# Six of eight rows of four down projections as pairs of seven products, and pairs that split two blocks at once

## The chip, the core and the metric

The kernel runs on one core of a Trainium2 chip. Its time is the device time of one execution in microseconds. Five engines work side by side: TensorE multiplies, ScalarE and VectorE prepare its operands and take its results out of PSUM, SyncE (SP) starts the plain weight loads, and GpSimd (POOL) starts those loads that are added to what is already in the buffer.

## The reference

One layer of each of two blocks, in float32, on 512 tokens of width 1024. What matters here are three feed-forward parts:

```python
def swiglu(x, w_gu, w_down):          # twice in the first block, D_FF = 2816
    g, u = jnp.split(x @ w_gu, 2, axis=-1)
    return (jax.nn.silu(g) * u) @ w_down
...
        x = x + jnp.square(jax.nn.relu(h @ w_up[l])) @ w_down[l]   # second block, width 4096
```

Between and around them stand a gated convolution, gated linear attention, neighbourhood attention, retention and norms, which keep their arithmetic.

## The kernel before

All activations lie transposed: 128 features on the partitions, 512 tokens along the row. Each float32 product is made of three float32r matmuls: the weight is split into a high part (`wh`, a cast on ScalarE, `hi`) and a low part (`wl`, a subtraction on VectorE, `lo`), the activation into `Ahi` and `Alo`, and high by high, high by low and low by high are added up in PSUM.

The work is a fixed list of units. A plain unit is one row of 128 outputs: eight blocks of 128 inputs, three matmuls of 512 tokens each, so 24. A *pair* is two rows at once. Its weights are taken as a 2 by 2 matrix of blocks (two rows, two halves of the inputs), the activations as another (two halves of the inputs, two halves of the tokens), and the product is made with seven block products instead of eight: `pair` on TensorE runs c = 0 to 6, each four inputs deep, with three matmuls of 256 tokens, so 84. The seven weight operands are a block, a sum s1, a sum s2, a block, a sum s3, a sum s4, a block. POOL loads s1 and s3 straight from memory, with a second load added on the way (`weight_sums`); VectorE makes s2 and s4 (`total`). `pair_hi` and `pair_lo` split one operand each, in 512 columns.

The results of a pair are collected in three PSUM banks. ScalarE copies three of them out on the way (`tap`, which TensorE waits for before it adds the next product into the same bank: c = 2 waits for tap 0, c = 4 for tap 2), VectorE adds others to the copies (`merge` 0 to 2; c = 6 waits for merge 1).

The gate and up projections of the FFNs, from the eighth (FFN 1) or sixth (FFN 2) row on, three gate projections of the mixer, and three of the four groups of the MLP's up projection run as pairs. For them the activation side is a normed input that is fixed for the whole layer, so the seven activation operands (`BThi`, `BTlo`) are built once ahead. The down projections run as plain units. An FFN works in groups of eight, eight and six hidden blocks (`FG`), the MLP in four groups of eight: up rows first, then eight down units that add into X.

In the MLP a pair gives two rows of hidden units. The first row's ReLU and square (`TA[3]`, `TA[4]`) follow merge 2, the second row's right half follows merge 1, and its left half follows the last product: `second_left` (a ReLU on ScalarE) stands in the *next* pair's queue, ahead of `tap(p, 0)`. `high` and `a_lo` split the result into `Ahi` and `Alo`.

Every engine's queue is written out by hand and runs in order; semaphores join them: `wh`, `wl` for splits, `pe` for products, `tp` for taps, `ev` for merges, `sd` for the sums, `ah`, `al` for activation splits. Weight buffers are a ring: three raw tiles, three tiles of high and three of low parts, each tile two half slots of 512 columns.

## Time and profile before

| | us |
|---|---|
| median of 3 runs | 1752.6 (1752.58 to 1753.64) |
| profiled execution | 1752.49 |
| its span, first to last instruction | 1750.3 |
| TensorE busy | 1743.7 |
| VectorE busy | 1180.2 |
| ScalarE busy | 847.5 |
| POOL busy | 201.8 |

The profile follows one execution. A row of a timeline gives the start, the duration, the engine, the line, what is written from what, the shape, how many instructions were merged into it, and in brackets how long the engine stood idle before it and what ended that. The shown duration of one instruction overlaps the next one's start by about a tenth of a microsecond, and matmul durations show the whole pipeline, so the distance between starts tells what an instruction costs its queue.

### The profile page before, as it was taken

The page shows a single profiled execution, that of the slowest core. Times are in us where ns is not written, and L with a number is a line of the kernel's source. Part 1 is how long each engine was busy: PE and PEld are TensorE (multiplying, and loading weights), DVE is VectorE, ACT ScalarE, POOL GpSimd, SP SyncE. Part 2 cuts the span into 40 slices and gives each one's busy share as a digit, 9 for nine tenths or more (in the row PEclk, how much of TensorE's full clock was granted, in tenths as well). Part 3 has the DMA queues.
Part 4 walks back from the last instruction along what each step waited for, and adds up shares of the span by engine and source line. Part 5 has one row for each costly group of instructions (what it writes and reads, how often), then busy time and mean ns, then how long its engine had stood idle before and what let it go on. Part 6 is the DMA issues. An engine that isn't in the chain of part 4 may idle for free.

```text
span 1750.3 us, 26650 instructions
## 1 busy us (share of the span) xinstructions
PE 1743.7 (100%) x10407; PEld 1534.1 (88%) x10407; DVE 1180.2 (67%) x1843; ACT 847.5 (48%) x1442; POOL 201.8 (12%) x262
## 2 busy tenths in 40 slices
PE   9999999999999999999999999999999999999998
PEld 7889989878888899988888998988877888989897
DVE  7848748666776546865794784876688677747474
ACT  6425526454333335743553562654655543727274
POOL 1002201000001012200110220200232010202000
PEclk9999999999999999999999999999999999999999
DMA  7247736332125355733445573634522253637352
GB/s 224 79 139 173 195 97 157 110 108 86 51 85 155 97 145 154 175 107 98 136 121 152 147 193 111 167 100 133 139 62 61 85 144 97 161 109 185 100 133 72
DMA packets 85451, 220.66 MB, mean 126 GB/s; under 512 B 10800, under 2 KB 12080, under 8 KB 85328
## 3 DMA queue, kind: packets, MB, share of 16 engines
q1 hardware_dynamic: 58512, 156.92, 29.1%
q0 software_dynamic: 25536, 59.97, 16.0%
q10 hardware_dynamic: 1280, 2.08, 0.3%
q8 instruction: 83, 1.36, 0.3%
q14 instruction: 40, 0.33, 0.1%
HBM read 214.74 MB, written 2.10 MB: 124 GB/s over the span
## 4 chain that ended last, share of the span: by engine, by line
PE 97%; DVE 1%; ACT 0%; issue 0%; DMA 0%; DVEq 0%; ACTq 0%; POOLq 0%
PE ps L2101 19%; PE ps L2103 19%; PE ps L2102 19%; PE ps L2193 10%; PE ps L2195 10%; PE ps L2194 10%; PE ps L2123 2%; PE ps L2125 2%; PE ps L2124 2%; PE ps L2342 0%; PE ps L2472 0%; PE ps L2497 0%; PE ps L2483 0%; PE ps L2345 0%; PE ps L2330 0%
## 5 line engine op out<-in xcount | busy, mean ns | idle before, releaser
L2101 PE MATMUL ps<-Ahi,wh 128*128 128x512 f32 x913 | 357.1, 391 | 0.0
L2102 PE MATMUL ps<-Alo,wh 128*128 128x512 f32 x913 | 355.3, 389 | 0.0
L2103 PE MATMUL ps<-Ahi,wl 128*128 128x512 f32 x913 | 355.3, 389 | 0.0
L2193 PE MATMUL ps<-BThi,wh 128*128 128x256 f32 x1232 | 340.2, 276 | 0.0
L2194 PE MATMUL ps<-BTlo,wh 128*128 128x256 f32 x1232 | 340.1, 276 | 0.0
L2195 PE MATMUL ps<-BThi,wl 128*128 128x256 f32 x1232 | 340.1, 276 | 0.0
L585 ACT ACTIVATE wh<-raw 128x1024 fp32r<-128x1024 f32 (+1 forms) x206 | 213.2, 1036 | 221.1 <-PE ps L2103 187.1
L1203 DVE TENSOR_TENSOR wl<-raw,wh 128x1024 fp32r<-128x1024 f32 (+1 forms) x206 | 250.2, 1215 | 64.4 <-ACT wh L585 62.3
L2194 PEld LDWEIGHTS ps<-BTlo,wh 128*128 128x128 f32 x1232 | 231.3, 188 | 0.0
L2193 PEld LDWEIGHTS ps<-BThi,wh 128*128 128x128 f32 x1232 | 231.3, 188 | 0.0
L2195 PEld LDWEIGHTS ps<-BThi,wl 128*128 128x128 f32 x1232 | 231.2, 188 | 0.0
L2103 PEld LDWEIGHTS ps<-Ahi,wl 128*128 128x128 f32 x913 | 171.4, 188 | 35.8
L2101 PEld LDWEIGHTS ps<-Ahi,wh 128*128 128x128 f32 x913 | 171.4, 188 | 35.7 <-issue 0.2
L2102 PEld LDWEIGHTS ps<-Alo,wh 128*128 128x128 f32 x913 | 171.4, 188 | 35.4 <-issue 0.2
L2101 PE MATMUL ps<-Hhi,wh 128*128 128x512 f32 x494 | 195.7, 396 | 0.0
L2103 PE MATMUL ps<-Hhi,wl 128*128 128x512 f32 x494 | 192.4, 390 | 0.0
L2102 PE MATMUL ps<-Hlo,wh 128*128 128x512 f32 x494 | 192.4, 389 | 0.0
L597 ACT ACTIVATE wh<-raw 128x512 fp32r<-128x512 f32 x168 | 105.0, 625 | 66.9 <-PE ps L2103 40.2
L1210 DVE TENSOR_TENSOR wl<-raw,wh 128x512 fp32r<-128x512 f32 x168 | 114.9, 686 | 7.8 <-ACT wh L597 6.5
L1294 DVE TENSOR_TENSOR tm<-ps,tm 128x256 f32<-128x256 f32 x168 | 71.0, 423 | 71.7 <-PE ps L2195 58.4
L2101 PEld LDWEIGHTS ps<-Hhi,wh 128*128 128x128 f32 x494 | 92.8, 188 | 22.1 <-issue 2.9
L2103 PEld LDWEIGHTS ps<-Hhi,wl 128*128 128x128 f32 x494 | 92.7, 188 | 19.6
(398 smaller groups left out, 2802.9 us busy)
## 6 DMA issues: line engine op xcount, KB each, us to landing
raw<-in_w_gu SPq DMA_DIRECT2D x96, 256.0 KB, 3.1
raw<-in_w_d SPq DMA_DIRECT2D x32, 512.0 KB, 4.2
raw<-in_w_dn SPq DMA_DIRECT2D x32, 512.0 KB, 4.1
raw<-in_w_gu SPq DMA_DIRECT2D x22, 512.0 KB, 3.8
raw<-in_w_up SPq DMA_DIRECT2D x36, 256.0 KB, 2.9
SS<-in_w_gu POOLq DMA_DIRECT2D x32, 256.0 KB, 5.1
tm<-in_w_gu POOLq DMA_DIRECT2D x32, 256.0 KB, 4.0
S1B<-in_w_gu POOLq DMA_DIRECT2D x32, 256.0 KB, 5.1
```

What stands on the lines that cost most here:

```text
L585: act.activation(WH[WS[u]][:, 0:n], RAW[RSL[u]][:, 0:n], ACT.Copy).then_inc(s["wh"], 1)
L597: act.activation(WHP[WS[p][c]], part(p, c), ACT.Copy).then_inc(s["wh"], 1)
L1203: dve.tensor_tensor(WL[WS[u]][:, 0:n], RAW[RSL[u]][:, 0:n], f32(WH[WS[u]][:, 0:n]), ALU.subtract).then_inc(s["wl"], 1)
L1210: dve.tensor_tensor(WLP[i], part(p, c), f32(WHP[i]), ALU.subtract).then_inc(s["wl"], 1)
L1294: dve.tensor_tensor(dst, BK[BANK[p][b]][:, LEFT], kept, ALU.add).then_inc(s["ev"], 1)
L2101: pe.matmul(ps, wh[:, c], hi[:, k, :], start=(k == 0), stop=False)
L2102: pe.matmul(ps, wh[:, c], lo[:, k, :], start=False, stop=False)
L2103: last = pe.matmul(ps, wl[:, c], hi[:, k, :], start=False, stop=(k == nb - 1))
L2123: pe.matmul(ps, Hhi[:, k, tc], wh[:, c], start=(k == 0), stop=False)
L2193: pe.matmul(ps, whi[:, w], bhi, start=(new and kp == 0), stop=False, skip_group_check=not new)
L2194: pe.matmul(ps, whi[:, w], blo, start=False, stop=False, skip_group_check=not new)
L2195: last = pe.matmul(ps, wlo[:, w], bhi, start=False, stop=(kp == 3), skip_group_check=not new)
```

## The change

The down projections of both FFNs' second group, and of the MLP's second and third groups, keep two plain rows and run the other six as three pairs. Their activation operands cannot be built ahead: the hidden blocks only arise in the up stage just before. Neighbouring blocks (0 and 1, 2 and 3, ...) take the two halves, so that a set can be built as soon as two blocks are there; the weights are laid out accordingly (`_mixed`, `column`). For each of four sets VectorE makes four blocks (`turned_ends`, `turned_middle`), ScalarE casts them (`turned_hi`), VectorE subtracts (`turned_lo`). In the FFNs these steps are spread over the up pairs 2 to 7 of the group and the first two down rows. In the MLP's pairs that begin at rows j = 2, 4 and 6 of a group VectorE makes the sums between `a_lo` of the second activation and merge 2, and ScalarE casts between the ReLU of the second row and that of the first. The fourth set is built during the first down row.

In all pairs the sums s1 and s2 lie beside each other, and so do s3 and s4, and each couple is split by one cast and one subtraction of 1024 columns: five steps (`STEP`) instead of seven. The ring of split weights grows from three tiles to four, temporaries shrink from nine to eight, and two FFN activations alternate between two temporaries. The space for descriptors of POOL's loads is halved. In every pair the casts stand in a new order around the taps.

```diff
-NW = 3
-NTMP = 9
+NW = 4
+NTMP = 8
...
+STEP = (0, 1, 1, 2, 3, 3, 4)
+NS = 5
+DOWN = ("w_d1", "w_d2", "w_dn")
+MIXED = (1, 2)
...
-                add(dn, n, a, b, 7)
+                add(dn, n, a, b, 7, a == FG[1][0] and n >= 2 and n % 2 == 0)
...
-            add("w_dn", n, 8 * g, 8 * g + 8, 7)
+            add("w_dn", n, 8 * g, 8 * g + 8, 7, g in MIXED and n >= 2 and n % 2 == 0)
...
-            wns = [w + c + 1 for c in range(NP)]
-            w += NP
+            wns = [w + k + 1 for k in range(NS)]
+            w += NS
+            while ws % 8 in (1, 3, 5, 6, 7):
+                slot(slot_free.get(ws % 8))
             got = [slot(p) for p in pens]
...
-    def part(p, c):
...
+        return SUM1[:, odd, :], SUM1[:, 2, :], SUM3[:, odd, :], SUM3[:, 2, :]
+
+    def part(p, k):
+
+        if k in (1, 3):
+            return (SUM1, SUM3)[k // 2][:, PAIR[p] % 2:3:2 - PAIR[p] % 2, :]
+        return RAWP[RSL[p][k // 2]]
+
+    def split(t, p, k):
+
+        i = WS[p][STEP.index(k)]
+        if k in (1, 3):
+            return t[:, 512 * i:512 * i + 1024].rearrange("p (i n) -> p i n", i=2)
+        return t[:, 512 * i:512 * i + 512]
 
     def added(p, i):
...
-        def pair_hi(p, c):
-
-            if c in (0, 3, 6):
-                i = c // 3
-                act.wait_ge(s[f"raw{RSL[p][i]}"], RN[p][i])
-            elif c in (1, 4):
-                act.wait_ge(*added(p, c if c == 1 else 3))
+        def pair_hi(p, k):
+
+            if k in (1, 3):
+                act.wait_ge(*added(p, k))
+                act.wait_ge(s["sd"], 2 * PAIR[p] + (k + 1) // 2)
             else:
-                act.wait_ge(s["sd"], 2 * PAIR[p] + {2: 1, 5: 2}[c])
-            act.wait_ge(s["pe"], WF[p][c])
-            act.activation(WHP[WS[p][c]], part(p, c), ACT.Copy).then_inc(s["wh"], 1)
+                act.wait_ge(s[f"raw{RSL[p][k // 2]}"], RN[p][k // 2])
+            if WF[p][k] > 0:
+                act.wait_ge(s["pe"], WF[p][k])
+            act.activation(split(WHF, p, k), part(p, k), ACT.Copy).then_inc(s["wh"], 1)
 
...
+        def turned_hi(i, kp):
+
+            act.wait_ge(s["tf"], 4 * i + kp + 1)
+            act.activation(THhi[:, kp, :, :], TF[:, kp, :, :], ACT.Copy).then_inc(s["th"], 1)
+
+        def down_pair(p):
+            v = p + 2
+            if p in DFIRST:
+                tap(p, 0)
+                pair_hi(p, 3)
+            else:
+                pair_hi(p, 3)
+                tap(p, 0)
+            pair_hi(p, 4)
+            tap(p, 1)
+            pair_next(v, 0)
+            tap(p, 2)
+            if v in PAIR:
+                pair_hi(v, 1)
+                pair_hi(v, 2)
+            else:
+                hi(v)
+                hi(v + 1)
+
         def operands(i, kp):
...
+                    if j == first:
+                        tap(p, 0)
+                        pair_hi(p, 3)
+                    else:
+                        pair_hi(p, 3)
+                        pair_a(j - 1, j - 1 - a)
+                        tap(p, 0)
                     pair_hi(p, 4)
-                    if j > first:
-                        pair_a(j - 1, j - 1 - a)
-                    tap(p, 0)
-                    pair_hi(p, 5)
-                    pair_hi(p, 6)
                     tap(p, 1)
                     pair_next(v, 0)
                     tap(p, 2)
-                    pair_next(v, 1)
                     if v in PAIR:
+                        pair_hi(v, 1)
                         pair_hi(v, 2)
-                        pair_hi(v, 3)
                     else:
                         hi(v)
                         hi(v + 1)
+                    if g == 1 and j - a in (4, 6):
+                        turned_hi(f, (j - a) // 2 - 2)
                     act.wait_ge(s["ev"], EV0[p] + 3)
                     act.activation(TA[3], TA[2], ACT.Silu).then_inc(s["silu"], 1)
                 pair_a(b - 1, b - 1 - a)
                 for n in range(KT):
...
                 p, v = MLP_UP[g] + j, MLP_UP[g] + j + 2
-                if j == 0:
-                    pair_hi(p, 4)
-                else:
+                pair_hi(p, 3)
+                if j > 0:
                     second_left(p - 2)
-                pair_hi(p, 5)
                 tap(p, 0)
-                pair_hi(p, 6)
+                pair_hi(p, 4)
                 tap(p, 1)
                 if j > 0:
                     high(j - 2, 3)
@@ -1113,19 +1173,19 @@
                     pair_hi(v, 0)
                 tap(p, 2)
                 if j > 0:
-                    high(j - 1, 5)
+                    high(j - 1, 7)
                 if v in PAIR:
                     pair_hi(v, 1)
                     pair_hi(v, 2)
-                    pair_hi(v, 3)
                 else:
                     hi(v)
                     hi(v + 1)
                 act.wait_ge(s["ev"], EV0[p] + 2)
                 if j > 0:
                     act.wait_ge(s["ah"], 60 + 8 * g + j)
-                own.add(act.activation(TA[5][:, RIGHT], TA[6][:, LEFT], ACT.Relu, scale=-1.0))
-                pair_next(v, 4)
+                own.add(act.activation(TA[7][:, RIGHT], TA[6][:, LEFT], ACT.Relu, scale=-1.0))
+                if g in MIXED and j > 0:
+                    turned_hi(1 + g, j // 2 - 1)
                 act.wait_ge(s["ev"], EV0[p] + 3)
                 own.add(act.activation(TA[3], TA[2], ACT.Relu))
                 own.wait()
@@ -1134,13 +1194,19 @@
                 high(6, 3)
                 second_left(p)
                 second_square(p)
-                high(7, 5)
+                high(7, 7)
             for n in range(KT - (g == 3)):
                 u = MLP_DN[g] + n
...
+        def turned_ends(kp):
+
+            e = TA[4][:, RIGHT].unsqueeze(1).broadcast_to([P, 2, 256])
+            two = TMF[:, 4 * (T + 8):4 * (T + 8) + 2 * (T + 264)].rearrange("p (i n) -> p i n", i=2)[:, :, LEFT]
+            own.add(dve.tensor_tensor(TF[:, kp, 0:4:2, :], two, e, ALU.subtract))
+
+        def turned_middle(kp):
+            t1, t2, t4 = (TF[:, kp, i, :] for i in (0, 1, 3))
+            own.wait()
+            own.add(dve.scalar_tensor_tensor(out=t2, in0=t1, scalar=-1.0, in1=TA[5][:, RIGHT], op0=ALU.mult,
+                                             op1=ALU.subtract))
+            own.wait()
+            dve.scalar_tensor_tensor(out=t4, in0=t2, scalar=-1.0, in1=TA[5][:, LEFT], op0=ALU.mult,
+                                     op1=ALU.subtract).then_inc(s["tf"], 1)
+
+        def turned_lo(i, kp):
+            dve.wait_ge(s["th"], 4 * i + kp + 1)
+            dve.tensor_tensor(THlo[:, kp, :, :], TF[:, kp, :, :], f32(THhi[:, kp, :, :]),
+                              ALU.subtract).then_inc(s["tl"], 1)
+
+        def down_last(p, scale):
+            n = UNITS[p][1] + 1
+            dve.wait_ge(s["pe"], PEN[p][6])
+            dve.scalar_tensor_tensor(out=X[:, n, LEFT], in0=BK[BANK[p][0]][:, LEFT], scalar=-scale,
+                                     in1=X[:, n, LEFT], op0=ALU.mult, op1=ALU.add).then_inc(s["ev"], 1)
+
+        def down_pair(p, scale):
+            n, v = UNITS[p][1], p + 2
+            if p not in DFIRST:
+                down_last(p - 2, scale)
+            pair_lo(p, 3)
+            pair_lo(p, 4)
+            if v in PAIR:
+                total(v, 2)
+                pair_lo(v, 0)
+            dve.wait_ge(s["ev"], EV0[p])
+            merge(p, 0, TA[2][:, LEFT])
+            merge(p, 1, TA[1][:, RIGHT])
+            dve.wait_ge(s["ev"], EV0[p] + 2)
+            own.add(dve.scalar_tensor_tensor(out=X[:, n + 1, RIGHT], in0=TA[1][:, RIGHT], scalar=-scale,
+                                             in1=X[:, n + 1, RIGHT], op0=ALU.mult, op1=ALU.add))
+            if v in PAIR:
+                pair_lo(v, 1)
+            else:
+                lo(v)
+            merge(p, 2, TA[2][:, RIGHT])
+            dve.wait_ge(s["ev"], EV0[p] + 3)
+            own.add(dve.scalar_tensor_tensor(out=X[:, n, :], in0=TA[2], scalar=scale, in1=X[:, n, :],
+                                             op0=ALU.mult, op1=ALU.add))
+            if v in PAIR:
+                total(v, 4)
+                pair_lo(v, 2)
+            else:
+                lo(v + 1)
+            if v not in DPAIRS:
+                down_last(p, scale)
+
         def to_h(base, n, g):
...
+                    if j > first:
+                        a_lo(38 * f + a, j - 1 - a, TA[4 + (j - 1) % 2])
                     pair_lo(p, 4)
-                    if j > first:
-                        a_lo(38 * f + a, j - 1 - a, TA[4])
-                    pair_lo(p, 5)
-                    pair_lo(p, 6)
+                    if g == 1:
+                        turned(j - a)
                     if v in PAIR:
+                        total(v, 2)
                         pair_lo(v, 0)
-                        total(v, 2)
                     merge(p, 0, TA[2][:, LEFT])
-                    if v in PAIR:
-                        pair_lo(v, 1)
                     dve.wait_ge(s["ev"], EV0[p])
                     merge(p, 1, TA[1][:, RIGHT])
                     if v in PAIR:
-                        pair_lo(v, 2)
+                        pair_lo(v, 1)
                     else:
                         lo(v)
                     merge(p, 2, TA[2][:, RIGHT])
                     if v in PAIR:
-                        pair_lo(v, 3)
                         total(v, 4)
+                        pair_lo(v, 2)
                     else:
                         lo(v + 1)
                 product(p, b - 1)
                 for n in range(KT):
                     u = DN[f, g] + n
+                    if u in PAIR:
+                        down_pair(u, 0.5)
+                    if u in PAIR or u - 1 in PAIR:
...
                 p, v = MLP_UP[g] + j, MLP_UP[g] + j + 2
+                pair_lo(p, 3)
                 pair_lo(p, 4)
-                pair_lo(p, 5)
-                pair_lo(p, 6)
+                if g in MIXED and j > 2:
+                    turned_lo(1 + g, j // 2 - 2)
+                if v in PAIR:
+                    total(v, 2)
                 if j > 0:
                     a_lo(60 + 8 * g, j - 2, TA[4])
                 if v in PAIR:
                     pair_lo(v, 0)
-                    total(v, 2)
                 merge(p, 0, TA[2][:, LEFT])
+                merge(p, 1, TA[6][:, LEFT])
                 if v in PAIR:
                     pair_lo(v, 1)
-                merge(p, 1, TA[6][:, LEFT])
-                if v in PAIR:
-                    pair_lo(v, 2)
                 else:
                     lo(v)
                 if j > 0:
-                    a_lo(60 + 8 * g, j - 1, TA[7])
+                    a_lo(60 + 8 * g, j - 1, TA[5])
+                    if g in MIXED:
+                        turned_ends(j // 2 - 1)
+                        turned_middle(j // 2 - 1)
                 merge(p, 2, TA[2][:, RIGHT])
                 if v in PAIR:
-                    pair_lo(v, 3)
                     total(v, 4)
+                    pair_lo(v, 2)
                 else:
                     lo(v + 1)
             for n in range(KT - (g == 3)):
                 u = MLP_DN[g] + n
+                if u in PAIR:
...
+            if p in DPAIRS:
+                if c in (0, 3, 5):
+                    k, half = {0: (2 * kp, LEFT), 3: (2 * kp + 1, LEFT), 5: (2 * kp + 1, RIGHT)}[c]
+                    return Ahi[:, k, half], Alo[:, k, half]
+                i = (1, 2, 4, 6).index(c)
+                return THhi[:, kp, i, :], THlo[:, kp, i, :]
...
-                pe.wait_ge(s["wl"], WN[p][c])
+                pe.wait_ge(s["wl"], WN[p][STEP[c]])
...
+                    if p in DFIRST and c == 1:
+                        pe.wait_ge(s["tl"], 4 * group_of(p) + kp + 1)
...
+def _mixed(t, groups):
+
+    for k in groups:
+        t[:, :, k:k + 8] = t[:, :, [k, k + 2, k + 4, k + 6, k + 1, k + 3, k + 5, k + 7]]
+    return t
+
...
-    nc = _bacc.Bacc("TRN2", target_bir_lowering=False, num_devices=1, dynamic_dma_scratch_size=4096)
+    nc = _bacc.Bacc("TRN2", target_bir_lowering=False, num_devices=1, dynamic_dma_scratch_size=2048)
```

## Rows read from the trace of the kernel before

**Rows 1.** The page: busy time by engine, and the granted clock in 40 slices.
```profile
PE 1743.7 (100%) x10407; PEld 1534.1 (88%) x10407; DVE 1180.2 (67%) x1843; ACT 847.5 (48%) x1442; POOL 201.8 (12%) x262
...
PEclk9999999999999999999999999999999999999999
```

**Rows 2.** The page: the chain of work that ended last, shares by engine.
```profile
PE 97%; DVE 1%; ACT 0%; issue 0%; DMA 0%; DVEq 0%; ACTq 0%; POOLq 0%
```

**Rows 3.** Timeline of VectorE, FFN 1's second down stage, additions to X.
```profile
223.63 0.69 DVE L1452 SCALAR_TENSOR_TENSOR X<-ps,X 128x512 f32<-128x512 f32 x1 [3.06 <-PE ps L2103]
...
229.07 0.69 DVE L1452 SCALAR_TENSOR_TENSOR X<-ps,X 128x512 f32<-128x512 f32 x1 [3.06 <-PE ps L2103]
```

**Rows 4.** Timeline of ScalarE, up pairs of the MLP's second group.
```profile
1497.88 0.39 ACT L613 ACTIVATE tm<-ps 128x256 f32<-128x256 f32 x1 [0.46 <-PE ps L2195]
...
1507.40 0.39 ACT L613 ACTIVATE tm<-ps 128x256 f32<-128x256 f32 x1 [0.33 <-PE ps L2195]
...
1513.51 0.64 ACT L1130 ACTIVATE tm<-tm 128x512 f32<-128x512 f32 x1
1514.17 0.64 ACT L1132 ACTIVATE tm<-tm 128x512 f32<-128x512 f32 x1
1514.71 0.37 ACT L1075 ACTIVATE tm<-ps 128x256 f32<-128x256 f32 x1
1514.98 0.63 ACT L597 ACTIVATE wh<-SW 128x512 fp32r<-128x512 f32 x1
```

**Rows 5.** Timeline of ScalarE, end of the same stage, a cast of 1024 columns.
```profile
1530.59 1.06 ACT L585 ACTIVATE wh<-raw 128x1024 fp32r<-128x1024 f32 x1 [0.93 <-PE ps L2195]
1531.55 0.40 ACT L1127 ACTIVATE tm<-tm 128x256 f32<-128x256 f32 x1
```

**Rows 6.** Timeline of VectorE, the MLP's first group: a subtraction of 1024 columns, dependent sums.
```profile
1425.16 1.22 DVE L1203 TENSOR_TENSOR wl<-raw,wh 128x1024 fp32r<-128x1024 f32 x1
1426.29 0.68 DVE L1347 TENSOR_TENSOR tm<-ps,R 128x512 f32<-128x512 f32 x1
...
1427.95 0.42 DVE L1264 TENSOR_TENSOR BF<-BF 128x256 f32<-128x256 f32 x1
1428.40 0.43 DVE L1266 SCALAR_TENSOR_TENSOR BF<-BF 128x256 f32<-128x256 f32 x1
1428.87 0.43 DVE L1268 SCALAR_TENSOR_TENSOR BF<-BF 128x256 f32<-128x256 f32 x1
```

**Rows 7.** Busy time by engine, the eight up pairs of FFN 1's second group.
```profile
core 0: us, PE busy (x) PEld busy (x) DVE busy (x) ACT busy (x) POOL busy (x), PEclk, DMA share, GB/s
139.56:215.70 76.14, 76.14 (x660) 75.61 (x659) 63.24 (x116) 47.19 (x91) 21.43 (x30) 1.00 0.81 196
```

**Rows 8.** Issue, median landing and use of a sum, the MLP's second group.
```profile
1506.57 0.93 POOL L533 DMA_DIRECT2D S1B<-in_w_up  x1
...
S1B<-in_w_up POOLq DMA_DIRECT2D x12, 256.0 KB, 5.6
...
1519.55 0.63 ACT L597 ACTIVATE wh<-S1B 128x512 fp32r<-128x512 f32 x1
```

**Rows 9.** Timelines of TensorE and ScalarE: a pair's first matmul and first tap.
```profile
256.11 0.29 PE L2193 MATMUL ps<-BThi,wh 128*128 128x256 f32 x1
...
257.69 0.39 ACT L613 ACTIVATE tm<-ps 128x256 f32<-128x256 f32 x1 [0.69 <-PE ps L2195]
```

**Rows 10.** Timeline of VectorE, up pairs of the MLP's second group.
```profile
1501.96 0.42 DVE L1294 TENSOR_TENSOR tm<-ps,tm 128x256 f32<-128x256 f32 x1 [0.34 <-PE ps L2195]
...
1512.46 0.68 DVE L1359 TENSOR_TENSOR Alo<-tm,Ahi 128x512 fp32r<-128x512 f32 x1
1513.06 0.41 DVE L1294 TENSOR_TENSOR tm<-ps,tm 128x256 f32<-128x256 f32 x1
```

**Rows 11.** Timeline of TensorE after a wait.
```profile
346.25 0.50 PE L2123 MATMUL ps<-wh,Hhi 128*128 128x512 f32 x1 [0.19 <-DVE wl L1203]
346.60 0.40 PE L2124 MATMUL ps<-wh,Hlo 128*128 128x512 f32 x1
```

More of the change, by code:

```diff
@@ L270, with interleaved, column, group_of @@
 END_FREE = [FREE[NU - 1] if i == 0 else _freed[b] for i, b in enumerate(END)]
+def interleaved(u):
+    name, n, k0, k1 = UNITS[u]
+    return name in DOWN and k1 - k0 == 8 and (k0 // 8 in MIXED if name == "w_dn" else k0 == FG[1][0])
+def column(u, k):
+    return k // 2 + k % 2 * 4 if interleaved(u) else k
+DPAIRS = [p for p in sorted(PAIR) if UNITS[p][0] in DOWN]
+DFIRST = [p for p in DPAIRS if p - 2 not in DPAIRS]
+def group_of(p):
+    return max(i for i, d in enumerate(DFIRST) if d <= p)
 def blocks(u):
@@ L628, in square @@
         def square(n):
-            act.activation(SS[:, :] if n == 0 else TA[n % 2], X[:, n, :], ACT.Square).then_inc(s["sq"], 1)
+            act.activation(SS if n == 0 else TA[n % 2], X[:, n, :], ACT.Square).then_inc(s["sq"], 1)
         def sums_hi(src, dst):
@@ L729, in after2 @@
             square(n)
-            act.activation(SS2[:, :] if n == 0 else TA[2 + n % 2], X[:, n, :], ACT.Square,
+            act.activation(SS2 if n == 0 else TA[2 + n % 2], X[:, n, :], ACT.Square,
                            scale=vc("gf", n)).then_inc(s["sq"], 1)
@@ L1079, in second_square @@
             own.wait()
-            act.activation(TA[7], TA[5], ACT.Square)
+            act.activation(TA[5], TA[7], ACT.Square)
         for g in range(4):
@@ L1221, in total @@
             if PREVP[p] is not None:
[L1222 to L1224 removed]
+                dve.wait_ge(s["wl"], WN[PREVP[p]][1 if i == 2 else 3])
             if i == 4:
@@ L1447, in ffn @@
                     u = DN[f, g] + n
+                    if u in PAIR:
+                        down_pair(u, 0.5)
+                    if u in PAIR or u - 1 in PAIR:
+                        continue
                     if n == 0:
-                        a_lo(38 * f + a, b - 1 - a, TA[4])
+                        a_lo(38 * f + a, b - 1 - a, TA[4 + (b - 1) % 2])
                     feed(u + 2)
+                    if g == 1 and n == 0:
+                        turned_ends(3)
+                        turned_middle(3)
+                    if g == 1:
+                        turned_lo(f, 2 + n)
                     dve.wait_ge(s["pe"], PEN[u])
@@ L1770, in dve_program @@
                 dve.wait_ge(s["rrow2"], 1)
-                own.add(dve.tensor_copy(SS2[:, :], BK[2][:, :]))
+                own.add(dve.tensor_copy(SS2, BK[2][:, :]))
                 own.wait()
@@ L2020, in dve_program @@
                 u = MLP_DN[g] + n
+                if u in PAIR:
+                    down_pair(u, 1.0)
+                if u in PAIR or u - 1 in PAIR:
+                    continue
                 if g > 0 and n == 0:
                     a_lo(60 + 8 * g, 6, TA[4])
-                    a_lo(60 + 8 * g, 7, TA[7])
+                    a_lo(60 + 8 * g, 7, TA[5])
                 feed(u + 2)
+                if g in MIXED and n == 0:
+                    turned_ends(3)
+                    turned_middle(3)
+                if g in MIXED:
+                    turned_lo(1 + g, 2 + n)
                 for step in BUILD_DN.get(n, ()) if g == 0 else ():
@@ L2089, in unit @@
             for k in range(nb):
-                c = slice(k * P, k * P + P)
+                c = slice(column(u, k) * P, column(u, k) * P + P)
                 if k == nb // 2 and mid:
@@ L2220, in ffn @@
                 for n in range(KT):
-                    if n == 0:
-                        unit(DN[f, g], Ahi, Alo, "al", 38 * f + a)
-                    else:
-                        unit(DN[f, g] + n, Ahi, Alo)
+                    u = DN[f, g] + n
+                    if u in PAIR:
+                        pair(u)
+                    elif n == 0:
+                        unit(u, Ahi, Alo, "al", 38 * f + a)
+                    elif u - 1 not in PAIR:
+                        unit(u, Ahi, Alo)
         def token_sums(col, src, last):
@@ L2564, in pe_program @@
             for n in range(KT - (g == 3)):
-                if n == 0:
-                    unit(MLP_DN[g], Ahi, Alo, "al", 60 + 8 * g)
-                else:
-                    unit(MLP_DN[g] + n, Ahi, Alo)
+                u = MLP_DN[g] + n
+                if u in PAIR:
+                    pair(u)
+                elif n == 0:
+                    unit(u, Ahi, Alo, "al", 60 + 8 * g)
+                elif u - 1 not in PAIR:
+                    unit(u, Ahi, Alo)
         wh, wl = WH[WS[NU - 1]], WL[WS[NU - 1]]
```

175 lines of the change are left out of this document (89 added, 86 removed).

## Prediction

> **What bounds the kernel now.** I read the page's busy times and its clock line first [rows 1]: TensorE is busy for 1743.7 of 1750.3 us, at a granted clock of nine tenths or more (2.4 GHz is the upper level) in every slice. The chain of waits says the same from behind: 97% of it is TensorE [rows 2]. So a change pays only if it takes matmul time out, and it costs only where it makes TensorE wait. The second question is therefore not how busy ScalarE and VectorE are, but how far ahead of TensorE's next wait each of their results stands.
>
> **What a pair takes out.** In a down stage each row of eight blocks adds its result to X every 5.44 us (229.07 - 223.63) [rows 3]: 24 matmuls of 512 columns, 0.2267 us each. Two rows are 10.88 us. A pair of seven products is 84 matmuls of 256 columns; the same tap of two consecutive pairs stands 9.52 us apart (1507.40 - 1497.88) [rows 4], which is 0.1133 us each and 1.36 us a product. One pair saves 1.36 us. Three pairs in each of four groups save 12 x 1.36 = 16.32 us if TensorE never waits.
>
> The rows show half the columns at exactly half the time, so no fixed cost per matmul. The Trainium skill, "TensorE: Matmul & The Clock Gate", section "Wait — 56ns, not 53.3ns?", puts a fixed 2.5 ns on every warm matmul; by its figures the two shapes would take 215.8 and 109.2 ns, an estimate of 10.36 us for two rows and 9.17 for a pair, 1.19 saved per pair and 14.3 in all. The measured rows decide here.
>
> **What is added, and where it is hidden in the FFNs.** Every pair of the kernel now splits two of its blocks with one instruction of 1024 columns. On ScalarE that is 0.95 us from start to next start (1530.59 to 1531.55) [rows 5], against two of 0.53 (one shows 0.63 at 1514.98 [rows 4], less the tenth by which 1.06 becomes 0.95); on VectorE 1.13 us (1425.16 to 1426.29) against two of 0.60 [rows 6]. That is a small saving of throughput, but the casts ahead of a tap are longer. Each new group also builds four sets of turned blocks from the activations: on VectorE `turned_ends` (512 columns; 0.74 us until the next may start, by 0.69 plus the hand-over seen below), two dependent operations of 0.47 us each (1427.95, 1428.40, 1428.87) [rows 6], and a subtraction of 1.13; on ScalarE a cast of 0.95, both priced as 1024 columns of a split.
>
> In the FFNs these are spread: sums for one pair of activations are made in the next two pairs, cast in a third, subtracted in a fourth. VectorE is busy 63.24 of 76.14 us over the eight pairs of FFN 1's second group [rows 7], 7.9 us a pair; summed by starts it is 7.7. The fullest new pair adds 0.81 + 1.13 and saves 0.14, so 9.5 of 9.52. It is the only one so full, and its merges would still come in time, because the turned work is queued before them with about a microsecond to spare. I take no cost; the bound above is 1 us per FFN. In the down pairs VectorE has no product or activation to split, about 7.6 us in 9.52. There a tap is queued behind a 1024-column cast, which waits for the fourth sum, behind the addition to X; I count 0.1 us of room. I take 0; if it were missed by 0.2 us in all ten places, 2 us.
>
> The first and second loads of a sum gate nothing new: an accumulation issued at 1506.57, landing 5.6 us later, is read at 1519.55 [rows 8], 7.4 us of room. The halved descriptor space for POOL's queue would have to delay a load by more than that; I take 0.
>
> The gates and the other groups keep their matmuls. Their reordered casts cost TensorE nothing by my count, 0.5 us at most.
>
> **Where it is not hidden: the MLP.** There is one long dependent chain in its second and third groups, and it closes on itself. I measure from the moment the previous pair's last product is released. A product is released 1.58 us after its first matmul starts (256.11 to 257.69) [rows 9], 1.36 plus 0.22; so product five is released at 6.80 (1501.96 is the merge that waits for it) [rows 10], and the third product of the next pair wants to start at 9.52 + 2.72 - 0.22 = 12.02. It must wait for the first tap of its own pair. After `merge(p, 1)` VectorE's queue now holds, ahead of `merge(p, 2)`: the two-block subtraction, the low part of the second activation, `turned_ends`, `turned_middle`. ScalarE's queue holds `turned_hi`, which waits for them, ahead of the ReLU and the square that read merge 2, and behind these stands the next pair's two-block cast, the left ReLU of this pair, and only then the tap. Step by step:
>
> merge 1 0.34, two-block subtraction 1.13, `a_lo` 0.60 (1512.46 to 1513.06) [rows 10], `turned_ends` 0.74, two middles 0.47 each, `turned_hi` 0.95, ReLU and hand-over 0.67 (1513.51 to 1514.17 is 0.66) [rows 4]: 5.37 from merge 1 to the square. Square 0.52, two-block cast 0.95, left ReLU 0.27 (1514.71 to 1514.98) [rows 4], tap with hand-over 0.43: 2.17. The tap is there at 6.80 + 7.54 = 14.34. TensorE waits 2.32 us in the pair after the first that builds.
>
> In the next pair the same happens, and now the wait shifts merge 1 too. Round the loop: from the third product's start three products to the release of the fifth, 3 x 1.36 + 0.22 = 4.30, another 0.15 because VectorE is then late by that, and 7.54: 11.99 per pair against 9.52. The last pair waits 2.47 us.
>
> Behind that the down projection waits. From merge 1 of the last pair to its square it is 5.37 again; then high part, left ReLU, its square, the high part of block seven (0.67, 0.52, 0.43, 0.67), the cast 0.67 and the subtraction 0.74 give 9.07. TensorE reaches that block 2.72 + 7 x 0.68 - 0.22 = 7.26 after merge 1: it waits 1.81 us, in two pieces. And the first down pair's second product wants the low part of the last turned set: from the start of that same subtraction VectorE needs 3.48 us to the turned sums (0.60 itself, a sum and a split of 0.60 each, 1.68 for the turned sums), ScalarE 0.95 and a 1024-column cast 1.10, VectorE another 3.61 (1.13 + 0.60 + 0.60 + 1.28), 9.14 in all; TensorE needs 0.74 + 0.68 + 5.44 + 1.36 = 8.22. Another 0.92.
>
> One group loses 2.32 + 2.47 + 1.81 + 0.92 = 7.52 us, two groups 15.04. The MLP's fourth group has no turned work, but its tap too is behind a cast of 0.95: merge 2 comes at 6.80 + 0.34 + 1.13 + 0.60, and 0.47 + 0.67 + 0.52 + 0.95 + 0.27 + 0.43 later the tap is done, 12.18 against 12.02, twice 0.16. Each of these twelve waits also shows the first weight load: after a wait TensorE's first two matmuls start 0.35 us apart (346.25, 346.60) [rows 11] instead of 0.23, 1.4 us in all. The sum is -16.32 + 15.04 + 0.32 + 1.4 = +0.4 us. The profiled execution took 1752.49 us for its span of 1750.3, 0.1 below the median of 1752.6, so I predict 1753.0 us.
>
> Each of the long waits is known to perhaps 0.4 us (`turned_ends` between one plain instruction's 0.60 and 0.75 with hand-over, the hand-overs of 0.05 each); eight of them make 3 us either way, 1750 to 1756 for this case alone.
>
> **The rivals.** (1) *The chain does not hold TensorE in the MLP.* For it: VectorE's work is 9.8 us in the fullest pair (4.1 of splits, 1.2 of sums, 1.2 of low parts, 1.0 of merges, 1.3 and 1.0 of turned work) and ScalarE's 8.5, so if the queues ran ahead, only 0.3 us would be lost. Against it: the tap stands behind a ReLU that needs merge 2, and that is queued behind the turned sums, so running ahead is impossible. With no loss the time is 1736.2; with half of the chain's cost, for instance because two of the steps overlap where I add them, about 1745. Decides at 4 us of 16 less wait than computed. (2) *The clock falls in the waits.* Nothing in the rows before shows a TensorE wait this long, and the granted clock is 1.00 in the stretch of [rows 7] and in no slice below nine tenths. If each of the four long waits were followed by one or two products at 1.2 GHz, twice the 1.36 us, that is 4 x 1.36 to 8 x 1.36, so 1758 to 1764. It decides from three such products on. The Trainium skill, "TensorE: Matmul & The Clock Gate", section "HAM oscillation — how this bites in real kernels", describes just this: gaps between bursts of matmuls after which the next burst runs at half rate. No row here shows it. (3) *The small margins go too:* down pairs, FFN pairs and gates each a few tenths late, 2 + 2 + 0.5 us, 1757. (4) *The sums' transfers are late* through the smaller descriptor space: a delay above 7.4 us per pair would show in all pairs; little speaks for it.
>
> **The numbers.** The forecast 0.60 (nearly all within 0.2%, which is 3.5 us and about what a measurement here tells from no change); rival 1 0.22, half of it near 1736 and half near 1745; rival 2 0.10; rivals 3 and 4 0.08 together. Faster than 1749.1: 0.23, with a little of the forecast's lower edge. Slower than 1756.1: 0.18. Within: 0.59. To leave out two in ten, the range runs from 1744, which takes in the half-hidden chain and leaves out 0.12, to 1758, which leaves out most of rival 2.
>
> **What would show it.** TensorE's waits by releaser should name ScalarE's tap copies twice per MLP group with 2.2 to 2.6 us each and nowhere else above 0.3 us; two waits for `Alo` at the first row of each MLP down stage with 0.9 us each; one of 0.9 us for the subtraction of the turned blocks. Both FFNs should be 4.08 us shorter each, with down pairs 9.52 us apart, and the two MLP groups each 3 to 4 us longer. ScalarE should stand idle about 3 us ahead of each turned cast in the MLP and not in the FFNs. Wrong would be: no tap wait in the MLP (rival 1), a stretch with a granted clock below 1.0 behind a wait (rival 2), or waits in the FFNs' down pairs (rival 3).

## Result and profile after the change

The changed kernel takes 1760.06 us (median of six runs, 1756.59 to 1762.07), the kernel before took 1753.01 us beside it: 1.0038 times as long, 95% interval 1.0027 to 1.0049. The forecast was 1753.0 us, with a range of 1744 to 1758; the measured time lies above both. The profiled execution took 1762.07 us for a span of 1760.3.

The page of the changed kernel, first the lines that answer to [rows 1] and [rows 2]: busy time by engine, the granted clock in 40 slices, the chain that ended last.

```profile
PE 1742.2 (99%) x10839; PEld 1551.8 (88%) x10839; DVE 1246.8 (71%) x1903; ACT 880.7 (50%) x1418; POOL 236.2 (13%) x310
PEclk9999999999999999999999999999999999999999
...
PE 45%; DVE 2%; ACT 1%; issue 1%; ACTq 0%; DVEq 0%
```

These lines hide what happened. TensorE is still "busy" for 99%, and its clock shows a nine in every slice, since 44 us are averaged in each. Nor does the chain help: its shares sum to 49% because it could be followed back over only half the span, so the fall of TensorE's share from 97 to 45% is no sign of waiting. The two largest entries of TensorE's list of waits are these (engine, line, releaser: us in total, times, longest).

```profile
PE ps L2344 <- ACT tm L648: 9.6, 7, 2.2
PE ps L2244 <- DVE Alo L1478: 1.7, 4, 0.5
```

L648 is the tap copy. Seven waits, of which four are about 2.2 us; the timeline puts these at the third product of the pairs `j = 4` and `j = 6` of both new MLP groups, as forecast. The other three (1.0 us together) stand in the gates (two) and in FFN 2's first pair.

What the four waits do to the clock is seen only in narrow windows around them (start, end and length, busy us of each engine with its instructions, PEclk, DMA share, GB/s).

```profile
1512.00:1515.60 3.60, 1.45 (x13) 1.26 (x12) 1.88 (x4) 3.57 (x7) 0.00 (x0) 1.00 0.18 60
1515.60:1519.00 3.40, 3.35 (x17) 3.38 (x18) 3.40 (x5) 2.91 (x7) 1.49 (x2) 0.55 0.56 117
1519.00:1525.50 6.50, 6.50 (x57) 6.50 (x57) 4.99 (x10) 2.41 (x5) 1.46 (x2) 0.97 0.74 157
1529.20:1532.70 3.50, 3.48 (x18) 3.50 (x19) 2.93 (x4) 2.55 (x7) 1.48 (x2) 0.55 0.44 119
1603.60:1604.70 1.10, 1.03 (x9) 1.06 (x10) 1.10 (x2) 1.10 (x3) 0.02 (x1) 0.99 0.00 0
1604.70:1608.10 3.40, 3.40 (x19) 3.40 (x17) 3.08 (x5) 3.02 (x6) 1.46 (x2) 0.50 0.63 104
1618.30:1621.70 3.40, 3.40 (x18) 3.40 (x17) 1.91 (x3) 2.54 (x5) 1.35 (x2) 0.50 0.75 184
```

In the first row TensorE stands still for 2.2 of 3.6 us; behind it, it runs at half its clock, the lower level of 1.2 GHz. TensorE does 17 to 19 matmuls in 3.4 us where it would do 30. The lost time, from start to start of these matmuls less 0.1133 us each, is 1.66, 1.68, 1.60 and 1.59 us: 6.5 us. After the waits that end at 1603.67 and 1617.30 the clock holds for another microsecond and then falls just the same. Away from these four places no stretch of the span, read in windows of 5 us, is below 0.98 before the last ten microseconds, and in the kernel before none is at all until its last five.

The ledger by stage, from the additions to X at the stages' ends (changed kernel less before): start +0.7 (0.6 of it in the first 8 us, around the wait for the first input, which differs from trace to trace, 0.2 to 1.2 us); FFN 1's second group -3.36; gates +1.25; rows up to FFN 2's first group, with its first pair, +1.36; FFN 2's second group -3.36; MLP +13.4. In the MLP that is -6.7 for six pairs, +11.6 waits, from the start before one to the start behind it less a matmul (9.2 for taps, 2.35 for `Alo`), +6.5 clock, +0.6 in the fourth group, and 1.4 more: 0.65 are a slower pace of the up pairs behind the waits, which comes back below, and some 0.6 are the second matmuls behind waits, which start 0.08 to 0.11 us late.

The chain itself, in the second pair of the MLP's second group, answering to [rows 4] and [rows 10]. First VectorE, from merge 1 to merge 2:

```profile
1508.05 0.42 DVE L1356 TENSOR_TENSOR tm<-ps,tm 128x256 f32<-128x256 f32 x1 [0.94 <-PE ps L2346]
1508.39 1.22 DVE L1275 TENSOR_TENSOR wl<-SUM,wh 128x1024 fp32r<-128x1024 f32 x1
1509.53 0.69 DVE L1478 TENSOR_TENSOR Alo<-tm,Ahi 128x512 fp32r<-128x512 f32 x1
1510.13 0.68 DVE L1362 TENSOR_TENSOR TF<-tm 128x512 f32<-128x512 f32 x1
1510.85 0.43 DVE L1367 SCALAR_TENSOR_TENSOR TF<-TF,tm 128x256 f32<-128x256 f32 x1
1511.31 0.42 DVE L1370 SCALAR_TENSOR_TENSOR TF<-TF,tm 128x256 f32<-128x256 f32 x1
1511.65 0.42 DVE L1356 TENSOR_TENSOR tm<-ps,tm 128x256 f32<-128x256 f32 x1
```

Then ScalarE, up to the tap, and the matmul that waited for it:

```profile
1511.77 1.06 ACT L657 ACTIVATE THhi<-TF 128x1024 fp32r<-128x1024 f32 x1 [2.83 <-DVE TF L1370]
1512.73 0.62 ACT L1190 ACTIVATE tm<-tm 128x512 f32<-128x512 f32 x1
1513.38 0.63 ACT L1192 ACTIVATE tm<-tm 128x512 f32<-128x512 f32 x1
1513.92 1.04 ACT L631 ACTIVATE wh<-SUM 128x1024 fp32r<-128x1024 f32 x1
1514.86 0.36 ACT L1137 ACTIVATE tm<-ps 128x256 f32<-128x256 f32 x1
1515.13 0.37 ACT L648 ACTIVATE tm<-ps 128x256 f32<-128x256 f32 x1
```

```profile
1515.65 0.36 PE L2344 MATMUL ps<-BThi,wh 128*128 128x256 f32 x1 [2.19 <-ACT tm L648]
```

From merge 1 to the square it is 5.33 us (5.37 forecast), from the square to the matmul's start 2.27 (2.17 to the tap's release). The order of the steps is the forecast's, one by one.

### The profile page after: what moved, and what is told of

Same layout as the page of the kernel before. It is cut to its first block and busy times, and to the rows that moved or that the text cites. A ratio compares the mean times of both kernels' runs of the same rounds, so it can differ in the third digit from the quotient of the medians.

```text
span 1760.3 us, 27645 instructions
## 1 busy us (share of the span) xinstructions
PE 1742.2 (99%) x10839; PEld 1551.8 (88%) x10839; DVE 1246.8 (71%) x1903; ACT 880.7 (50%) x1418; POOL 236.2 (13%) x310
## 5 line engine op out<-in xcount | busy, mean ns | idle before, releaser
L2244 PE MATMUL ps<-Ahi,wh 128*128 128x512 f32 x721 | 282.8, 392 | 1.7 <-DVE Alo L1478 1.7
L2245 PE MATMUL ps<-Alo,wh 128*128 128x512 f32 x721 | 280.7, 389 | 0.0
L2246 PE MATMUL ps<-Ahi,wl 128*128 128x512 f32 x721 | 280.7, 389 | 0.0
L1269 DVE TENSOR_TENSOR wl<-raw,wh 128x1024 fp32r<-128x1024 f32 (+1 forms) x182 | 221.0, 1216 | 40.7 <-ACT wh L620 39.0
L620 ACT ACTIVATE wh<-raw 128x1024 fp32r<-128x1024 f32 (+1 forms) x182 | 186.0, 1031 | 46.5 <-PE ps L2246 31.5
L631 ACT ACTIVATE wh<-SUM 128x1024 fp32r<-128x1024 f32 x136 | 143.9, 1058 | 104.5 <-DVE SUM L1290 59.2
L1275 DVE TENSOR_TENSOR wl<-SUM,wh 128x1024 fp32r<-128x1024 f32 x136 | 165.8, 1219 | 33.5 <-ACT wh L631 33.5
L2244 PEld LDWEIGHTS ps<-Ahi,wh 128*128 128x128 f32 x721 | 135.3, 188 | 31.5 <-DVE Alo L1478 3.4
L2246 PEld LDWEIGHTS ps<-Ahi,wl 128*128 128x128 f32 x721 | 135.3, 188 | 28.4
L2245 PEld LDWEIGHTS ps<-Alo,wh 128*128 128x128 f32 x721 | 135.4, 188 | 27.8 <-issue 0.2
```

The source lines that it names most:

```text
L620: act.activation(WH[WS[u]][:, 0:n], RAW[RSL[u]][:, 0:n], ACT.Copy).then_inc(s["wh"], 1)
L631: act.activation(split(WHF, p, k), part(p, k), ACT.Copy).then_inc(s["wh"], 1)
L1269: dve.tensor_tensor(WL[WS[u]][:, 0:n], RAW[RSL[u]][:, 0:n], f32(WH[WS[u]][:, 0:n]), ALU.subtract).then_inc(s["wl"], 1)
L1275: dve.tensor_tensor(split(WLF, p, k), part(p, k), f32(split(WHF, p, k)), ALU.subtract).then_inc(s["wl"], 1)
L2244: pe.matmul(ps, wh[:, c], hi[:, k, :], start=(k == 0), stop=False)
L2245: pe.matmul(ps, wh[:, c], lo[:, k, :], start=False, stop=False)
```

## Experiments

**The clock against the wait: two kernels that do more work.** The theory: each long wait costs twice, once as a wait and once as a fall of the clock behind it. The rivals: the falls are incidental (A), or much shorter waits bring them too (B). In the four pairs that wait, TensorE computes its second product (or first and second) twice before releasing it. The repeated matmuls only fill the wait.

```
-                for kp in range(4):
+                for kp in (0, 1, 2, 3) * (2 if c in again else 1):
...
-                    pair(MLP_UP[g] + j)
+                    pair(MLP_UP[g] + j, (1,) if g in MIXED and j > 2 else ())
```

> In the four MLP pairs in which TensorE waits 2.2 us for the first tap, the second product is computed twice before it is released: 4 x 12 matmuls (5.4 us of work) more, the result unchanged, and some 0.85 us left of each wait. Theory (the clock falls behind a long wait, 1.6 to 1.7 us each in the changed kernel's rows): no stretch under 1.00 in the MLP, 1760 - 6.5 = 1753.5 us, faster although it does more work. Rival A (the waits alone cost, the falls are incidental): the work fits into the waits, so 1760 +- 0.5 us and the falls stay. Rival B (a wait of 0.85 us is enough for a fall): 1760 us too, but with waits of 0.85 us ahead of each fall.

> The same with the first and the second product computed twice: 2.72 us of repeated matmuls for a wait of 2.36 us with its restart, so no wait is left and 4 x 0.36 = 1.4 us of matmul are added. Theory: clock 1.00 throughout the MLP, 1760 - 6.5 + 1.4 = 1755 us. Rival A: 1761.5 us with falls. Rival B: 1755 us here, as the theory, but 1760 in the kernel with one repeated product.

Measured: 1755.35 us with the second product repeated (ratio to before 1.0014, 1.0006 to 1.0023), 1756.42 with both (1.0019, 1.0010 to 1.0028). With 48 more matmuls, 5.4 us of work, the kernel is 4.7 us faster than the changed one. The waits of the first, and its clock in the same stretch of the MLP:

```profile
PE ps L2344 <- ACT tm L648: 4.3, 7, 0.8
```

```profile
1515.00:1520.00 5.00, 4.87 (x43) 4.90 (x44) 5.00 (x9) 4.74 (x10) 1.49 (x2) 1.00 0.57 158
1520.00:1530.00 10.00, 9.17 (x81) 9.00 (x80) 8.20 (x12) 7.14 (x14) 2.94 (x4) 1.00 0.67 160
1530.00:1535.00 5.00, 5.00 (x42) 4.83 (x41) 3.90 (x8) 1.97 (x3) 0.86 (x1) 1.00 0.79 195
```

Waits of 0.83 us are left and no fall follows them. Rival A is out, and so is rival B. Both kernels stand above the theory's numbers, by 1.9 and 1.4 us, and the 4.7 us are less than the profiled execution's 6.5. One reason is on record: the changed kernel's six runs have mean granted clocks from 0.996 (1762.07 us) to 0.999 (1756.59), so it seems that not every wait is followed by a fall in every run, and their spread of 5.5 us goes with the clock; a trace exists of the first run alone. Two repeated products cost 1.07 us more than one, near the 1.4 computed.

**The FFNs alone.**

```
-MIXED = (1, 2)
+MIXED = ()
```

> Down pairs in the two FFNs alone; the MLP keeps its rows of eight in the down projections, but the new order and the two-block splits stay everywhere. Theory (a down pair saves 1.12, not 1.36 us; the gates' and other pairs' reordered casts cost 2.6 us; the MLP's up pairs 0.3 us each at two pairs in three groups): 1752.5 - 6.7 + 2.6 + 1.8 = 1750 us. Rival (the prediction's own steps: 1.36 a pair, the reordering nothing): 1752.5 - 8.2 + 0.5 = 1745 us. Rival (the whole loss is in the FFNs or the reordering): above 1753 us.

Measured: 1750.61 us (0.9987, 0.9978 to 0.9995), the theory's number. The down pairs help where nothing waits for them, but less than the forecast's 1.36 us a pair, and the reordering around them is not free.

**The same instructions in the MLP, in another order.** Nothing is added or removed; the turned sums are made while VectorE waits for products anyway, and ScalarE squares early and casts the turned sums where no merge waits behind them. The core of both loops:

```
 ScalarE: second_left(p - 2); pair_hi(p, 3); square into TA[4]; tap(p, 0);
          high(j - 2); second_square(p - 2); pair_hi(p, 4); high(j - 1); tap(p, 1); tap(p, 2);
          pair_hi(v, 0..2); turned_hi; ReLU of merge 1; ReLU of merge 2
 VectorE: pair_lo(p, 3); total(v, 2); a_lo(j - 2); pair_lo(p, 4); a_lo(j - 1); turned_ends;
          pair_lo(v, 0); merge 0; turned_middle; merge 1; pair_lo(v, 1); merge 2;
          total(v, 4); pair_lo(v, 2); turned_lo
```

> The changed kernel with the same instructions in the MLP's up loops in another order: ScalarE squares ahead of the first and second tap and casts the turned sums last; VectorE makes the turned sums ahead of the second merge, in the time in which it waited for the products. Theory (the loss is the chain that runs through the first tap, plus the clock behind it): tap waits under 0.2 us, no fall, no wait for the first down row; 12 x 1.12 = 13.4 us saved, 2.6 lost in the gates: 1741 to 1743 us. Rival (VectorE's 9.8 us of work in 9.52 bind whatever the order): 0.3 to 1 us in each of four pairs, 1743 to 1746 us. Rival (the turned sets cost as work, not as order): above 1752 us.

Measured: 1742.74 us (0.9941, 0.9928 to 0.9953): 17.3 us less than the changed kernel, by order alone. Its waits of TensorE:

```profile
PE ps L2517 <- DVE ones L1740: 1.1, 1, 1.1
PE ps L2347 <- ACT tm L648: 1.0, 3, 0.4
```

The four MLP waits and those for `Alo` are gone, and with them every fall of the clock; the three small tap waits outside the MLP have stayed. VectorE's amount of work, which the first rival named, does not bind.

**The three small waits.** One of them in the changed kernel: ScalarE's casts of merged blocks (L948) stand ahead of the third tap in its queue and wait for VectorE's product L1831, which stands late in its own queue.

```profile
702.89 0.63 ACT L948 ACTIVATE Hhi<-tm 128x512 fp32r<-128x512 f32 x1
704.15 0.63 ACT L948 ACTIVATE Hhi<-tm 128x512 fp32r<-128x512 f32 x1 [0.63 <-DVE tm L1831]
704.69 0.36 ACT L648 ACTIVATE tm<-ps 128x256 f32<-128x256 f32 x1
```

```profile
705.20 0.36 PE L2344 MATMUL ps<-MThi,wh 128*128 128x256 f32 x1 [0.40 <-ACT tm L648]
```

On top of the reordered kernel the third tap moves ahead of those casts, and in the FFNs the fourth sum of the first pair ahead of VectorE's wait for a product:

```
             pair_next(v, 0)
+            tap(p, 2)
             for r in SPLITS.get(k, ()):
...
-            tap(p, 2)
...
+                    if j == JS[f] - 1:
+                        total(u + 2, 4)
                     dve.wait_ge(s["pe"], PEN[u + 1])
```

> The reordered kernel, and in the gates the third tap ahead of the casts of the merged blocks, in the FFNs the fourth sum of the first pair ahead of the wait for a product. Theory (the reordering's 2.6 us are these three late taps of 0.66, 0.66 and 0.46 us with what follows them): no tap wait over 0.1 us anywhere, 1742.7 - 2.6 = 1740 us. Rival (the reordering costs elsewhere as well): between 1741 and 1742.7 us.

Measured: 1740.49 us (0.9936, 0.9918 to 0.9954), 2.25 less, and the fastest version of the study. Ten of its eleven runs lie between 1739.47 and 1742.56 us. The other, which is in the ratio and is the profiled one, took 1758.71 us at a granted clock of 0.95 from its beginning to its last microseconds, so its rows give no times to compare; its list of waits has no tap any more.

**No down pair at all**, with the same reordering and early taps (`DOWN = ()`, `MIXED = ()`, and no turned blocks):

> No down pair at all, all else as in the kernel with reordered MLP loops and earlier taps: the two-block splits and the new order stay. If a down pair is worth 1.12 us and nothing is lost around the twelve, 1740.5 + 13.4 = 1753.9 us; if it is worth 1.36 us, 1756.8 us. If the splits and the order by themselves cost nothing any more, it should stand within 1 us of the kernel before.

Measured: 1752.13 us (0.9996, 0.9987 to 1.0005). So the two-block splits and the new order cost nothing once no tap is late, and the twelve pairs are worth 11.6 us, 0.97 each, below both numbers expected. Each taken against the kernel before beside it (1753.26 and 1753.64 us), they are worth 12.0.

**Why a pair is worth less than 1.36 us.** In the changed kernel, FFN 1's second group, the same addition to X in two consecutive down pairs:

```profile
231.82 0.42 DVE L1397 SCALAR_TENSOR_TENSOR X<-tm,X 128x256 f32<-128x256 f32 x1
...
241.58 0.43 DVE L1397 SCALAR_TENSOR_TENSOR X<-tm,X 128x256 f32<-128x256 f32 x1
```

9.76 us, not 9.52, with no wait between. By TensorE's starts the products that read halves of `Ahi` and `Alo` take 1.42 us, those that read turned blocks 1.36 to 1.38. The distance to the next start counts a product's last matmul with the product behind it; three products of 1.44 and four of 1.36 make the 9.76. This stood in the kernel before, in the gate pairs, which read halves too (merge 1 of three consecutive ones, VectorE):

```profile
708.91 0.42 DVE L1294 TENSOR_TENSOR tm<-ps,tm 128x256 f32<-128x256 f32 x1 [0.24 <-PE ps L2195]
...
718.67 0.43 DVE L1294 TENSOR_TENSOR tm<-ps,tm 128x256 f32<-128x256 f32 x1 [0.30 <-PE ps L2195]
...
728.43 0.42 DVE L1294 TENSOR_TENSOR tm<-ps,tm 128x256 f32<-128x256 f32 x1 [0.30 <-PE ps L2195]
```

Is it the half, or the place? Weights, `Ahi` and `Alo` lie at 128 within 512 bytes, the up pairs' and the turned blocks at 64. Four kernels move one or the other by 64 bytes; the first two start from the reordered kernel, the last two have the earlier taps as well:

```
-    THhi, _ = sb("THhi", [P, 4, 4, 256], F32R, off=oHhi + 448)
+    THhi, _ = sb("THhi", [P, 4, 4, 256], F32R, off=oHhi + 512)
...
```

```
     Hlo, oHlo = sb("Hlo", [P, KT, T], F32R)
-    EBD, _ = sb("EBD", [P, 4, 4, 8])
+    at[0] += 448
     Ahi, oAhi = sb("Ahi", [P, KT, T], F32R)
     Alo, oAlo = sb("Alo", [P, KT, T], F32R)
+    at[0] += 64        (the fourth kernel alone)
     RAWS, _ = sb("raw", [P, NRAW, 1024])
...
```

> The kernel with the reordered MLP loops, with the turned blocks of the down pairs 64 bytes further on in SBUF (at the same place within 512 bytes as the activations, 128 where they were at 64, as the up pairs' blocks are). Theory (the pace of a 256-column product depends on where its moving block lies: 1.36 to 1.38 us at 64, 1.42 at 128): the four products of a down pair that read turned blocks take 1.42 too, a pair 9.94 instead of 9.76 us, 12 x 0.18 = 2.2 us more, 1745 us. Rival (a product that reads half of a 512-wide row is slower, wherever the row lies): no change, 1742.7 us.

> The same reordered kernel with the activations' high and low parts 64 bytes lower in SBUF (at 64 within 512 bytes, as the up pairs' blocks), a small table moved out of the way. Theory (place): the products that read halves of the activations take 1.36, a down pair 9.52 us, 12 x 0.24 = 2.9 us less; the twelve gate pairs, which read the same tensor, 2.9 less too: 1737 us. Rival (half rows): 1742.7 us.

> All three at once: MLP loops reordered, taps of gates and first FFN pairs earlier, activations 64 bytes lower. If the three terms are separate: 1742.7 - 2.6 - 5.8 = 1734 us; if the place does nothing: 1740 us.

> Reordered MLP loops and earlier taps, and the activations 64 bytes lower in SBUF while the weights stay where they were, so that the two no longer lie at the same place within 512 bytes (64 against 128). Theory (a 256-column product is slow when its moving block and its weights lie at the same such place, as the rows of the two runs before suggest: 1.44 us in every product where both lay at 128, and where both lay at 64): the half-row products take 1.36, a down pair and a gate pair 9.52 us, 24 x 0.24 = 5.8 us less than 1740.5: 1734.7 us. Rival (half rows are slow in any place): 1740.5 us.

Measured: 1746.38, 1779.75, 1778.88 and 1765.17 us. The first agrees in kind, larger than expected (+3.6 us): with the turned blocks at 128 all seven products of a down pair take 1.44, 12 x (10.08 - 9.76) = 3.8 us. The other three times went far the other way from what I expected. In the second and third run, the weights, which lie behind the activations, moved along with them, to 64, where the up pairs' blocks are too. FFN 1's up pairs in 50 us of TensorE without a wait, first in the changed kernel, then in the second of the four:

```profile
150.00:200.00 50.00, 50.00 (x444) 50.00 (x443) 44.56 (x77) 32.64 (x54) 15.38 (x21) 1.00 0.79 199
```

```profile
150.00:200.00 50.00, 50.00 (x419) 50.00 (x418) 42.04 (x72) 30.71 (x51) 14.44 (x20) 1.00 0.77 187
```

444 matmuls against 419, at a granted clock of 1.00. In the fourth run, weights at 128 and activations at 64, it is the rows of 512 columns that are slow: additions to X in FFN 1's first down stage are 5.60 us apart, against 5.44.

```profile
104.35 0.69 DVE L1594 SCALAR_TENSOR_TENSOR X<-ps,X 128x512 f32<-128x512 f32 x1 [3.77 <-PE ps L2252]
109.95 0.69 DVE L1594 SCALAR_TENSOR_TENSOR X<-ps,X 128x512 f32<-128x512 f32 x1 [3.77 <-PE ps L2252]
```

Yet its first down pair (FFN 1) does what was expected of it. All its seven products take 1.36 us; the same stretch of the changed kernel, also within down pairs and without a wait, is the second row.

```profile
228.00:240.00 12.00, 12.00 (x109) 12.00 (x108) 8.67 (x15) 5.76 (x10) 2.94 (x4) 1.00 0.47 113
```

```profile
228.00:240.00 12.00, 12.00 (x105) 12.00 (x104) 10.39 (x18) 6.88 (x13) 4.23 (x6) 1.00 0.70 180
```

From 249.93 on, behind a matmul that starts 0.08 us late, its products take 1.41 us, as those of the up pairs ahead of it and behind it do.

So the place in SBUF sets the pace, of one operand against the other, and not the half by itself. At the two places tried, 64 and 128, all these traces agree: with moving block and weights at the same place 12 matmuls of 256 columns take 1.44 us and 12 of 512 columns 2.72; with the two apart it is 1.36, or the 1.41 just named, and 2.75 to 2.80. `Ahi` is read both ways. The shift wins the 0.24 us a pair only until the slower pace sets in, and loses more in rows of 512 columns and up pairs.

## Why the prediction was wrong, step by step

**What bounds the kernel** held: the time followed TensorE's matmuls and waits to the end.

**The long dependent chain in the MLP** was right in place, order and size: tap waits in the pairs forecast, 2.15 to 2.36 us from start to start against 2.32 and 2.47 and a restart of 0.12 forecast. The waits behind it were sized too large: 1.18 us a group for `Alo` instead of 1.81, and none of 0.92 for the turned blocks. With the late second matmul behind each, waits and restarts of the two groups are 12.3 us against some 16 forecast.

**"The clock falls in the waits" was the step that failed.** It stood as rival 2 with a chance of 0.10, and the forecast took nothing for it, for the reason that no row before shows a wait that long. That was no evidence for a steady clock: the change was forecast to make just such waits. Its price, 4 x 1.36 to 8 x 1.36, contains the measured 6.5 us. That its time, 1758 to 1764, contains the measured one too is partly luck, since the other errors nearly cancel. Waits and restarts came out some 4 us smaller, the pairs saved 2.9 us less, and gates with FFN 2's first group, start and pace added 2.6, 0.7 and 0.65. The Trainium skill, "TensorE: Matmul & The Clock Gate", section "HAM oscillation — how this bites in real kernels", describes bursts that run at half rate after a gap; the rows agree in kind, with gaps of 2.2 us, shorter than in its example, and granted clocks of 0.50 to 0.55 behind them, and the repeated products show it by experiment. With the falls gone and the waits mostly filled the kernel stands at 1755.35, inside the range.

**"Each pair saves 1.36 us" was mis-sized.** The FFN stages are 3.36 us shorter each, 1.12 a pair; over twelve pairs 2.9 us less. The pace was taken from up pairs, whose seven products all read blocks of their own. The nearest row was the gate pair's, whose products read halves of a wide tensor as the down pair's do; it stood in the trace at 9.76 us. What makes the difference is the place of the halves in SBUF, by the displaced kernels.

**"The gates cost nothing, 0.5 us at most" was wrong by 2 us:** three late taps, two in the gates (1.25 us) and one in FFN 2's first pair (1.36, of which 0.9 are the slower pace that follows it), removed by moving two steps (2.25 us).

**The FFNs' margins held:** no wait in any down pair, nor in the up pairs of the two second groups. Rivals 1, 3 and 4 did not occur, except that rival 3's gates did. The MLP's fourth group lost 0.3 us a pair against 0.16.

The sum with measured terms is -13.4 + 11.6 + 6.5 + 0.6 + 2.6 + 0.7 (start) + 1.4 (pace and restarts) = +10.0 us, as much as between the two spans; the two profiled executions are 9.6 apart.

**Left open:** why the place in SBUF sets two paces, and what starts and ends the third, 1.41 us, which the fourth displaced kernel's up pairs have though their blocks and weights lie as before.

## What to carry to other kernels

Where a change is forecast to make TensorE wait longer than any wait in the trace, price the clock behind the wait as well as the wait, and do not take nothing for it because no row shows such a wait yet. When new work costs more than its share, look first for the dependent step that was queued ahead of the next release: the same instructions in another order were worth 17 us here. Take a product's pace from the rows that read operands of the same shape and from the same tensor.

## What was unexpected of the hardware

Matmuls of equal shape at a granted clock of 1.00 have more than one pace. 12 of 256 columns take 1.36 or 1.44 us, depending on where the two operands lie in SBUF (above), and 1.41 depending on what came before. The kernel before and the one without down pairs run every up stage at 1.36 from its second product on. In the changed kernel the late tap of FFN 2's first pair is followed by 1.41 to the end of that up stage; first the kernel before, then the changed one:

```profile
910.00:930.00 20.00, 20.00 (x179) 20.00 (x178) 15.56 (x29) 11.13 (x22) 6.11 (x9) 1.00 0.84 201
```

```profile
910.00:930.00 20.00, 20.00 (x172) 20.00 (x172) 14.81 (x26) 11.89 (x19) 6.63 (x9) 1.00 0.82 195
```

All six traces with this late tap show it, two of them 7 us later, behind a matmul that starts 0.08 us late. A small wait can therefore cost more behind it than in itself: 0.37 us here, and 0.9 of pace. It need not, for the waits of 0.83 us that the repeated product leaves are followed by 1.36. And the slower pace needs no wait: in the reordered kernel's third MLP group TensorE goes from 1.36 to 1.41 us a product at about 1591 and stays there to the end of the up stage, with no wait in the list.

```profile
1575.00:1590.00 15.00, 15.00 (x134) 15.00 (x134) 13.04 (x22) 11.92 (x23) 4.72 (x7) 1.00 0.86 205
1590.00:1605.00 15.00, 15.00 (x130) 15.00 (x129) 14.04 (x24) 13.71 (x26) 4.40 (x6) 1.00 0.61 149
```

134 and 130 matmuls in equal time, TensorE busy throughout. In the MLP this makes the reordered kernel's six pairs worth 5.5 us instead of 6.7 (the stage from the last row of the first group to the first of the fourth is 201.4 us against 206.9 without pairs). What starts the slower pace was not tried.
